# Down projection of a gated MLP on one core: 24 rounds of a seven-product scheme in place of 96 plain weight units

## What is computed

```python
def hybrid_block(x):                       # one layer, x (1, 512, 2048)
    h = rmsnorm(x, norm_mix_pre)
    y = hybrid_mixer(h, ...)               # 16 attention heads and 16 recurrent blocks, @ w_out
    x = x + rmsnorm(y, norm_mix_post)
    h = rmsnorm(x, norm_ffn_pre)
    g = causal_dwconv(h @ w_gate, conv_ffn_w, conv_ffn_b)
    y = (gelu(g) * (h @ w_up)) @ w_down    # hidden width 6144, w_down (6144, 2048)
    return x + rmsnorm(y, norm_ffn_post)
```

## Time and profile before

| | us |
|---|---|
| runs (3) | 2187.03 to 2187.22, median 2187.09 |
| span of the profiled execution | 2186.0 |
| PE busy | 2171.7 (99%), 18942 matmuls |
| DVE busy | 1529.4 (70%) |
| ACT busy | 1002.2 (46%) |
| POOL busy | 141.7 (6%) |
| HBM read, written | 306.09 MB, 21.00 MB |

### The profile page before, as it was taken

The page is one execution under the profiler, slowest core; times in us unless marked ns, Lnnn a source line. Parts: engine busy times, 40 slices in busy tenths (PEclk is TensorE's granted clock), DMA queues, the critical chain, the costliest instruction groups (busy, mean ns, idle before and its releaser), DMA issues.

```text
span 2186.0 us, 45684 instructions
## 1 busy us (share of the span) xinstructions
PE 2171.7 (99%) x18942; PEld 2154.4 (99%) x18942; DVE 1529.4 (70%) x2030; ACT 1002.2 (46%) x1278; POOL 141.7 (6%) x210
## 2 busy tenths in 40 slices
PE   9999999999999999999999999999999999999998
PEld 8999999999999999999999999999999999999998
DVE  7776777778755977888888888888885444444445
ACT  6555555447322554444444444444443343343433
POOL 0000000000100001111111111111111100000000
PEclk9999999999999999999999999999999999999999
DMA  5222222222432437777777777777767632222343
GB/s 175 91 99 94 85 92 95 89 96 87 150 112 97 163 116 203 209 214 210 209 203 206 209 206 207 209 214 204 204 178 219 192 113 97 96 96 96 99 170 116
DMA packets 100850, 329.01 MB, mean 151 GB/s; under 512 B 13024, under 2 KB 20832, under 8 KB 100208
## 3 DMA queue, kind: packets, MB, share of 16 engines
q1 hardware_dynamic: 75456, 240.06, 31.9%
q0 software_dynamic: 22672, 82.36, 17.5%
q10 hardware_dynamic: 2592, 4.72, 0.6%
HBM read 306.09 MB, written 21.00 MB: 150 GB/s over the span
## 4 chain that ended last, share of the span: by engine, by line
PE 97%; DVE 2%; ACT 1%; issue 0%; POOL 0%; DVEq 0%; ACTq 0%; POOLq 0%
PE bank L1816 31%; PE bank L1818 31%; PE bank L1817 31%; PE bank L1901 1%; PE bank L1914 1%; PE bank L1926 0%; DVE x_b L1807 0%; PE bank L1925 0%; PE bank L1986 0%; ACT w_all L589 0%; DVE w_all L1058 0%; PE bank L1872 0%; PE bank L2004 0%; PE bank L2003 0%; PE bank L1932 0%
## 5 line engine op out<-in xcount | busy, mean ns | idle before, releaser
L1816 PE MATMUL bank<-act_hi,w_all 128*128 128x256 f32 x2832 | 786.3, 278 | 1.7 <-DVE act_lo L1530 0.9
L1818 PE MATMUL bank<-act_hi,w_all 128*128 128x256 f32 x2832 | 782.2, 276 | 0.0
L1817 PE MATMUL bank<-act_lo,w_all 128*128 128x256 f32 x2832 | 782.1, 276 | 0.0
L1816 PEld LDWEIGHTS bank<-act_hi,w_all 128*128 128x128 f32 x2832 | 531.6, 188 | 5.4 <-issue 2.5
L1817 PEld LDWEIGHTS bank<-act_lo,w_all 128*128 128x128 f32 x2832 | 531.7, 188 | 0.4
L1818 PEld LDWEIGHTS bank<-act_hi,w_all 128*128 128x128 f32 x2832 | 531.6, 188 | 0.0
L1816 PE MATMUL bank<-w_all,act_hi 128*128 128x256 f32 x1536 | 424.0, 276 | 0.1
L1818 PE MATMUL bank<-w_all,act_lo 128*128 128x256 f32 x1536 | 423.9, 276 | 0.0
L1817 PE MATMUL bank<-w_all,act_hi 128*128 128x256 f32 x1536 | 423.9, 276 | 0.0
L1068 DVE TENSOR_TENSOR w_all<-raw,w_all 128x1024 fp32r<-128x1024 f32 x95 | 116.4, 1226 | 279.5 <-ACT w_all L595 279.5
L1816 PEld LDWEIGHTS bank<-w_all,act_hi 128*128 128x128 f32 x1536 | 288.3, 188 | 0.3 <-issue 0.3
(11 more groups left out here) (297 smaller groups left out, 3707.0 us busy)
## 6 DMA issues: line engine op xcount, KB each, us to landing
raw<-weights SPq DMA_DIRECT2D x310, 512.0 KB, 3.3
raw_s<-weights SPq DMA_DIRECT2D x84, 512.0 KB, 5.0
raw_s<-weights POOLq DMA_DIRECT2D x84, 512.0 KB, 5.7
raw_a<-weights SPq DMA_DIRECT2D x42, 512.0 KB, 5.5
h_spill<-h_out POOLq DMA_DIRECT2D x48, 256.0 KB, 3.4
h_t<-h_spill POOLq DMA_DIRECT2D x24, 512.0 KB, 4.1
x<-xT POOLq DMA_DIRECT2D x16, 256.0 KB, 3.9
out<-x ACTq DMA_DIRECT2D x16, 256.0 KB, 2.3
```

Source lines behind the costliest of these rows:

```text
L1816: pe.matmul(dst, ah, bh, start=start, stop=False, skip_group_check=goes_on)
L1817: pe.matmul(dst, ah, bl, start=False, stop=False, skip_group_check=goes_on)
L1818: return pe.matmul(dst, al, bh, start=False, stop=stop, skip_group_check=goes_on)
```

## The change

The down projection becomes 24 more rounds of the same loop (NF = NS + ND = 42 + 24). The hidden width is cut in three blocks of 16 tiles (CH = 3); for each block there are eight rounds, one for each pair of output tiles. In a round the weights are the stationary operand again, and y comes out channel by partition, as everything else does. The seven activation operands of a block (two quadrants and five combinations, each 128 x 2048, 1 MB) are formed by VectorE from pairs of hidden tiles as these come out (`t_of_pair`, `t3_of_pair`), stored to DRAM (`t_spill`) by GpSimd's queue, and loaded for a block when the places of the block before come free (`load_t`): there are eight places for seven operands. Each is then converted (high part on ScalarE, low part on VectorE; for operands 5 and 6 on GpSimd), behind a product's weights in the order that `T_AFTER` gives.

Two of the weight sums that the scheme needs (A21 + A22 and A21 + A11) are made in DRAM during the head pairs, by GpSimd's queue: for each of 24 rounds two copies and two accumulating transfers. Other weight quadrants of a round are read from the old layout with rows of 512 B. y of the first block is stored to DRAM, that of the second added there by an accumulating store, and the result is loaded back into SBUF, where VectorE adds the third. The squares are summed as tiles come out; the end has one root, one spread over the partitions, 16 operations that scale, 16 additions of x1 (12 on GpSimd, 4 on VectorE) and 16 stores. The transposes are gone. The semaphores of the forget gate are merged, without a change in what waits for what.

The core of the diff:

```diff
+CH = 3
+CK = UK
+PAIRS_OUT = KT // 2
+ND = CH * PAIRS_OUT
+NF = NS + ND
+HT = FT // 2
+T_PLACE = {0: 0, 2: 1, 4: 2, 5: 3, 3: 4, 1: 5, 6: 6}
+ADD_BY_DVE = (3, 8, 12, 15)
+T_BY_POOL = (5, 6)
+T_AFTER = {1: 5, 2: 6, 3: 7, 4: 8, 5: 9, 6: 10}
...
+        OPERANDS = ((P00, T0, T1, T2, P10, P11, T3), (P01, P00, T0, T1, T2, P10, P11), (T3, P01, P00, T0, T1, T2, P10),
+                    (P11, T3, P01, P00, T0, T1, P10))
...
+        def t_free_after(c, n):
+            last = N_FAST + 7 * (NS - 1 + PAIRS_OUT * c)
+            if n == 0:
+                return last - 7 if c else N_FAST
+            return last + 7 if c == CH - 1 and n == 6 else last + n
...
+        def down_weights(i, r, kh):
+            c, o = (i - NS) // PAIRS_OUT, (i - NS) % PAIRS_OUT
+            u, n = U_DOWN + o // 2 * PER_GROUP + CK * c, o % 2 * 2 * P + r * P
+            return weights[u:u + CK].rearrange("u p (t n) -> t p u n", t=2)[kh][:, :, n:n + P]
...
         @block.sync
-            for i in range(NS):
+            for i in range(NF):
...
+                if i < NS:
+                    sp.dma_start(raw[:, 0], weights[u]).then_inc(a11_landed, 16)
+                else:
+                    sp.dma_start(in_k(raw[:, 0]), down_weights(i, 0, 0)).then_inc(a11_landed, 16)
...
+            for t in range(KT):
+                sp.wait_ge(x1_stored, 16 * KT)
+                sp.wait_ge(unit_used, N_FAST + 7 * (NF - 1) + 1 + t // 8)
+                sp.dma_start(x1_place(t), in_two(out[:, t])).then_inc(x1_back, 16)
...
         @block.gpsimd
+            def copy_for_sums(n):
+                for k in range(2):
+                    pool.dma_start(in_k(s_d[n, k]), down_weights(NS + n, 1, 0)).then_inc(s_copied, 16)
+            def add_for_sums(n):
+                pool.wait_ge(s_copied, 32 * n + 32)
+                pool.dma_start(in_k(s_d[n, 0]), down_weights(NS + n, 1, 1), accum_op=ALU.add).then_inc(s_added, 16)
+                pool.dma_start(in_k(s_d[n, 1]), down_weights(NS + n, 0, 0), accum_op=ALU.add).then_inc(s_added, 16)
+            def sums(n0, n1):
+                for n in range(n0, n1):
+                    if n:
+                        pool.wait_ge(s_added, 32 * n)
+                    copy_for_sums(n)
+                    add_for_sums(n)
+            sums(0, 2)
+            for p in range(1, NP):
                 pool.wait_ge(gw_split, p)
+                pool.dma_start(gw[:], gate_w[p]).then_inc(gw_landed, 16)
                 pool.wait_ge(s_taken, p * 6)
+                pool.dma_start(negc[:], negc_d[2 * p:2 * p + 2].partition_broadcast(P)).then_inc(negc_landed, 16)
+                sums(3 * p - 1, 3 * p + 2)
+            sums(3 * NP - 1, ND)
...
+            def load_t(c, n):
+                pool.wait_ge(unit_used, t_free_after(c, n))
+                m = CK * (c + 1)
+                for stored_t, each in ((to_stored, 16), (te_stored, 16), (tq_stored, 32), (t3_stored, 16)):
+                    pool.wait_ge(stored_t, each * m)
+                pool.dma_start(operand(NS + PAIRS_OUT * c, n)[3], t_d[c, T_PLACE[n]].rearrange("p (k n) -> p k n", n=HS)).then_inc(t_landed[n], 16)
+            def lo_of_t(c, n):
+                pool.wait_ge(th_done, 7 * c + n + 1)
+                hi, lo, _, summed = operand(NS + PAIRS_OUT * c, n)
+                pool.tensor_tensor(lo, summed, word(hi), ALU.subtract).then_inc(tp_split, 1)
...
+            for i in range(NF):
+                if i <= NS:
+                    store_after(PLAIN - 1 + i)
...
+                c, o = (i + 1 - NS) // PAIRS_OUT, (i + 1 - NS) % PAIRS_OUT
+                if i > NS and i - 1 < NS + 2 * PAIRS_OUT:
+                    store_y(i - 1)
+                if i >= NS - 2 and c + 1 < CH and o == PAIRS_OUT - 1:
+                    load_t(c + 1, 0)
+                if i >= NS - 1 and c < CH and o == 0:
+                    for n in range(1, 6):
+                        load_t(c, n)
+                    if c == CH - 1:
+                        load_y(0)
+                        load_y(1)
+                    load_t(c, 6)
+                    for n in T_BY_POOL:
+                        lo_of_t(c, n)
...
+                pool.tensor_tensor(x1_place(t), x1_place(t), in_two(Y_TILES[t]), ALU.add).then_inc(taken_p, 1)
...
         @block.vector
+            def t_of_pair(m):
+                e, o = h_out[:, 0], h_out[:, 1]
+                qa, qb = q_place(m)
...
+                dve.tensor_tensor(qa, o[:, HS:], e[:, HS:], ALU.subtract)
+                dve.tensor_tensor(e[:, HS:], e[:, 0:HS], e[:, HS:], ALU.subtract).then_inc(te_ready, 1)
...
+            def t_n_lo(c, n):
+                dve.wait_ge(th_done, 7 * c + n + 1)
+                if n in T_BY_POOL:
+                    return
+                hi, lo, _, summed = operand(NS + PAIRS_OUT * c, n)
+                dve.tensor_tensor(lo, summed, word(hi), ALU.subtract).then_inc(tn_split, 1)
+            def t_n_after(i, n, convert):
+                k = 7 * (i - (NS - 1)) + n
+                for c in range(CH):
+                    if k == 7 * PAIRS_OUT * c - 2:
+                        convert(c, 0)
+                    for m in range(1, 7):
+                        if k == 7 * PAIRS_OUT * c + T_AFTER[m]:
+                            convert(c, m)
...
+                y = Y_TILES[t]
+                dve.scalar_tensor_tensor(out=y, in0=y, scalar=col("g_ffn_post", t), in1=banks[1][:], op0=ALU.mult,
+                                         op1=ALU.mult).then_inc(z_done, 1)
```

More of the change, by code:

```diff
@@ L164, in block_kernel @@
                       for part in range(2)]
-        level = w_all[:, LINE // 4:4 * UW + LINE // 4].rearrange("p (b x) -> p b x", b=2)
-        wd_hi, wd_lo = [[level[:, :, S * c:S * c + S] for c in (2 + part, part)] for part in range(2)]
         banks = [ctx.enter_context(nc.psum_tensor(f"bank{i}", [P, S], F32)) for i in range(8)]
@@ L1040, in _ @@
-            act.activation(y_s[:, 0:1], eps[:, 0:1], ACT.Sqrt).then_inc(y_std_done, 1)
-            act.wait_ge(y_std_done, 1)
-            act.wait_ge(y_summed, 3)
-            for i in range(QT):
-                down_square(GROUPS - 1, i)
-                if i:
-                    scale_last(i - 1)
-                token_root(i)
-            scale_last(QT - 1)
+                hi(i, 4)
+                if i <= NS:
+                    gelu_gate(j - 1)
+                if y_pair >= 0:
+                    y_square(y_pair + 1, c21_done)
@@ L1051, in _ @@
+            act.wait_ge(sum_done, 6)
+            act.activation(cols[:, 0], banks[0][:, 0:QT], ACT.Sqrt, scale=1.0 / D).then_inc(root_done, 1)
         @block.vector
@@ L1805, in _ @@
-            for k in range(KT):
-                dve.wait_ge(lifted, k + 1)
-                dve.scalar_tensor_tensor(out=x1_b[:, k], in0=banks[k % 8][:], scalar=col("g_ffn_post", k),
-                                         in1=x1_b[:, k], op0=ALU.mult, op1=ALU.add).then_inc(taken, 1)
+                if i <= NS:
+                    t_after(j - 1)
+                if square >= 0:
+                    add_y_square(square + 1)
+                lo(i, 5)
+                stage_free(i)
+                c22_of(i)
@@ L1872, in channel_sum @@
                     last = pe.matmul(bank[:], ones[:], src, start=(i == 0), stop=(i == len(srcs) - 1))
-                last.then_inc(sum_done, 1)
-            def column_sum(bank, src):
-                for j in range(QT):
-                    last = pe.matmul(bank[:, j:j + 1], src[:, P * j:P * j + P], ones[:, 0:1], start=True, stop=True)
                 last.then_inc(sum_done, 1)
@@ L2298, in _, with column_sums @@
-            for k in range(4, KT):
-                at_least(pe, taken, k - 7)
-                for i in range(QT):
-                    last = lift(k, i)
-                last.then_inc(lifted, 1)
+                fast_product(i, 5, c, False)
+                fast_product(i, 6, b, False)
+            def column_sums(src, j0, j1, stop):
+                for j in range(j0, j1):
+                    last = pe.matmul(banks[0][:, j:j + 1], src[:, P * (j - j0):P * (j - j0) + P], ones[:, 0:1],
+                                     start=src is acc and j == 0, stop=stop, skip_group_check=True)
+                return last
@@ new lines, in _ @@
+            pe.wait_ge(yacc_added, KT - 2)
+            column_sums(acc, 0, QT, False)
+            pe.wait_ge(ysq2_done, KT - 2 + 3)
+            column_sums(pu, QT // 2, QT, False)
+            column_sums(sq[:, 1], 0, QT, False)
+            pe.wait_ge(ysq2_done, KT - 2 + 4)
+            column_sums(pv, 0, QT // 2, True).then_inc(sum_done, 1)
+            for n in range(2):
+                c = slice(HS * n, HS * n + HS)
+                pe.wait_ge(diag_done, 3 + n)
+                pe.matmul(banks[1][:, c], ones[:], raw_s24[:, c], start=True, stop=True).then_inc(spread_done, 1)
```

735 lines of the change are left out of this document (373 added, 362 removed).

## The result

The changed kernel takes 2204.89 us, the median of four runs from 2203.84 to 2205.93. The kernel before took 2187.11 beside it (2187.03 to 2187.22). The ratio is 1.0081, with a 95% interval of 1.0068 to 1.0095, so it is slower, by more than the noise. The forecast was 2157, with a range of 2131 to 2182.

The account below looks back on a forecast made before the run. TensorE was taken to be bound by its count of matmuls. The profiled 2186.0 -65.6 (down projection) +31.7 (block changes) +4.0 (end) gave 2156.1; the runs' median lies 1.1 above the span, so 2157 us, range 2131 to 2182.

Parts of the forecast that it names:

- -65.6 for the matmuls: Down projection: 24 rounds of 19.04 us, 457.0 us, replace 522.6, saving 65.6 us if TensorE never waits.
- +31.7 for the block changes: Three block changes: late operand landings of 5.7, 7.9 and 12.5 us plus 5.6 of VectorE backlog, 31.7 us in all.
- The 5.7 of the second block: Second block's change: operand 6 lands 14.8 us after its place came free, against 9.1 allowed, so 5.7 us late.
- the term of the third, 7.9: Third block's change: operand 6, loadable only after the whole round and two tiles of partial sums, lands 7.9 us late.
- In the first it waits for landings anyway: First block's change: no VectorE backlog was added, whereas the second and third got 2.8 us each.
- POOL's subtractions, 0 and 4.6 us each: Block changes: GpSimd's subtractions of two operands take 4.6 us each and add 0 us to the kernel.
- Rival 1: Block changes: GpSimd's subtractions make VectorE's two-SBUF-input subtractions stand still, 3 x 4.6 = 14 us more, 2171; chance 0.22.
- Weight sums, T = 19 and cost 0: Head pairs: each weight sum in DRAM takes 19 us in GpSimd's queue, nothing is late, cost 0 us.
- Rival 3: Head pairs: weight sums come late in GpSimd's queue and delay gate weights and negc, 48 us at T = 24, 2205; chance 0.16.
- The rounds before the blocks, 0: Seven-product rounds: extra half-width VectorE operations, 1 us a round, and two more stores are hidden, 0 us.
- The end, +4.0: After TensorE's last matmul: 21.5 us instead of 17.5, with GpSimd's 12 additions at 1.15 us each, 4.0 us more.
- Rival 2: Block changes: hidden, with loads at 2.9 us each and ScalarE's lead carrying the rest, +9 us, 2134; chance 0.17.

Follow-up runs that it names:

- Run 1: The changed kernel without the operands' loads, conversions and subtractions at the three block changes, and without TensorE's waits for them: 2136.67 us.
- run 4: The changed kernel with the load of each block's operand 0 issued three to four rounds earlier in GpSimd's queue: 2187.62 us.
- run 5: The kernel of run 4 with the first block's loads of operands 1 to 5 issued before the store that waits for h_out: 2180.17 us.
- run 9: The kernel of run 6 with every operand's conversion and subtraction one product later: 2163.44 us.
- run 10: The kernel of run 9 with no low part of an operand formed, the high part taken instead: 2142.59 us.
- run 7: The kernel of run 5 with the low parts of operands 5 and 6 formed nowhere, the high part taken instead: 2158.56 us.
- run 3: The changed kernel with all seven low parts of a block on VectorE, none on GpSimd: 2195.53 us.
- run 6: The kernel of run 5 with all low parts on VectorE: 2170.82 us.
- run 2: The kernel before with the 24 weight sums made in DRAM as in the changed kernel, their results read by nobody: 2188.41 us.

## Why the prediction was wrong

- **-65.6 for the matmuls: right.** Run 1 has 24 rounds of 19.04 us.
- **+31.7 for the block changes: wrong, 70.2** (38.0, 11.8 and 20.3 for 12.5, 8.5 and 10.7), beyond the 55 that the prediction gave as a sign of being wrong. This is the step that failed, in three places; POOL's subtractions, the next point, are a fourth.
  - The count began with operand 1. Operand 0's load and conversion were not in it, though its DMA stands in the same queue, and as for operand 1 I asked only when ACT could go on, not what DVE has queued behind the subtraction, an eviction that PE waits for. Moving that one load gives 17.3 us (run 4), moving five loads in front of a store 7.4 (run 5). The store was in the working: it put the start of the loads at -9.5 instead of -16.3. What it meant for DVE was not.
  - The loads were pictured as one behind the other, 4.4 us each, the first landing after 6.4 and operand 6 of the second block 14.8 after its place came free. They overlap instead: in the second block the six land 6.0 to 9.5 us after issue, in the third 8.7 to 11.4 (medians of all 21: 8.8 and 9.3 in the DMA view). So they lie around the slack of 9.1, by at most 2.3 beyond it. The 5.7 of the second block were not there (ACT's waits for landings are 1.94 and 1.11), while the term of the third, 7.9, has its counterpart in the 6 us that run 9 gives back there.
  - "In the first it waits for landings anyway": DVE's own backlog, 5.6 us in the prediction for five subtractions a block on DVE, is 20.8 us for seven with the conversions a product later (runs 9 and 10), and the first block has it like the others. A product leaves DVE 2.72 us and asks 1.22 + 2.29.
- **POOL's subtractions, 0 and 4.6 us each: the cost was wrong.** 4.6 was near (5.6 with the waiting in it, 4.5 of work), but the price was 21.6 us (run 7). **Rival 1's mechanism is the true one**; its 14 counted only one of the two subtractions of a block, while either holds DVE up by some 4 us, and 2 x 4 x 3 = 24 is nearer to the 21.6. The view "on DVE they would cost 5 more a block" had the wrong sign: putting them there saves 9.4 (runs 3 and 6).
- **Weight sums, T = 19 and cost 0: right** (17.8 to 20.3; run 2). The second pair's gate weights landed 3.0 us after ACT was ready for them, and PE didn't wait. **Rival 3** named 2205, and the kernel takes 2204.9, but by coincidence: POOL issued negc at most 3.1 us later than before (152.84 for 149.75), against 32.5 of room.
- **The rounds before the blocks, 0: off by 3.1 us.** Set beside the rows of before, ACT's rows are 0.9 us late at the start of the plain hidden tiles, which run 2 shows too, with 0.8, so that this part comes with the sums. They are 2.8 late from 808 on. In between PE waits four times, 1.8 us in all, for DVE's subtraction of a plain unit (line 1181), where before it waited not at all, and what DVE has more to do there is the new work on pairs of hidden tiles. The prediction looked for this work's cost in the seven-product rounds only, where it is hidden. A last 0.4 comes at the first rounds, where DVE waits 4.55 us for a raw_s, for 4.03 before.
- **The end, +4.0: 8.7.** The first scaling comes after 4.7 us, not 3.8; POOL's additions take 16.5 us for 12, 1.38 each for the 1.15 of the select's rate; 4.0 for the last store, not 3.2.
- **Rival 2** (changes hidden) fell. It would need the subtractions gone: run 10 is at 2142.6.

By size: of the 68 us, 25 are the queue's order, 22 the two subtractions on POOL, which shut DVE out (the same two on DVE would be 12), 7 the landing slack (measured with all low parts on DVE), 6 the loads and ACT's conversions themselves (run 10 against run 1), and the remaining 8 to 9 I put down to DVE's five other subtractions a block, which by themselves were not measured. These are differences between kernels changed one after another and would shift with another order. Putting the eviction in front of the operand's subtraction in DVE's program was not tried.

## What to carry to other kernels

When a change inserts work into an in-order program, list for each engine what is queued behind the new wait, evictions included, and start with the very first insertion: one load issued 3 us after its consumer was ready, and landing 8.5 us after that, cost 15 us of TensorE. If VectorE is the helper that has no time left, moving two-input SBUF work to GpSimd doesn't relieve it; price it as VectorE time at GpSimd's duration (here 4 us of VectorE for each 4.5 of GpSimd). A saving of matmuls is kept only if the helpers' work for each product fits the product's time: here a third of the saving goes to subtractions even in the best order found.

## What was not expected of the hardware

- A GpSimd subtraction of 128 x 2048 fp32 takes 4.5 us, and VectorE's two-input operations beside it show its time as their own duration: 5.24 for 1.22, 5.04 for 0.75. The wait isn't shown as idle time, so a table of waits misses it; the mean of line 1822 (1294 ns for `w_all<-raw_s` in this kernel, 1224 with all on DVE) is where it shows.
- A gap of 9 to 13 us brought the granted clock to 0.50, and some 22 matmuls behind it ran at that level, 0.213 us apart: about 2 us a gap.
- 96 transfers of 512 KB from DRAM to DRAM with rows of 512 B, at a DMA share of 0.85, left TensorE busy for 499.3 of 500 us; by run 2 they cost the kernel at most 3 us.
